# Paired down projections by seven block products: where the weight differences are kept, and weight chunks loaded in halves

## The reference

```
h2 = modulate(rms_norm(x, g_pre_ffn), shift_f, scale_f)
ff = (silu(h2 @ w_ffn_gate) * (h2 @ w_ffn_up)) @ w_ffn_down
x  = x + gate_f * rms_norm(ff, g_post_ffn)
```

## Time and profile before

| | |
|---|---|
| median of 3 runs | 2852.0 us (2851.5 to 2852.65) |
| the profiled execution's own time | 2855.09 us |
| its span, first to last instruction | 2853.3 us |
| PE busy | 2725.7 us, 96% |
| DVE busy | 1694.5 us, 59% |
| POOL busy | 1648.9 us, 58% |
| ACT busy | 903.4 us, 32% |
| pair stage, units 1 to 22 | 2273.7 to 2739.3 us of the span |

### The profile page before, as it was taken

How to read it: one execution, slowest core, us unless ns; L and a number is a source line. 1 busy time by engine, 2 the same in 40 slices (tenths; PEclk the granted TensorE clock), 3 DMA queues, 4 the chain that set the end, 5 groups by cost and what they waited for, 6 DMA issues and landing times.

```text
span 2853.3 us, 38214 instructions
## 1 busy us (share of the span) xinstructions
PE 2725.7 (96%) x13018; PEld 2165.8 (76%) x13018; DVE 1694.5 (59%) x2404; ACT 903.4 (32%) x1776; POOL 1648.9 (58%) x1253
## 2 busy tenths in 40 slices
PE   8999999898999999999999999989999999999988
PEld 5777777686878888887788887768777787777767
DVE  6666687747567777777633203665274456556647
ACT  5544444535211111214222125553242122121112
POOL 4566311366987777765433252213458977777764
PEclk9999999999999999999999999999999999999999
DMA  4322221044111121133411342213433111111124
GB/s 143 100 89 90 89 89 52 8 148 159 38 60 52 47 64 44 59 115 128 173 45 51 97 159 82 82 34 140 152 117 114 33 59 45 45 59 44 44 97 169
DMA packets 76676, 243.35 MB, mean 85 GB/s; under 512 B 7135, under 2 KB 11008, under 8 KB 76164
## 3 DMA queue, kind: packets, MB, share of 16 engines
q1 hardware_dynamic: 54464, 183.78, 20.3%
q10 hardware_dynamic: 22084, 57.86, 5.7%
HBM read 206.48 MB, written 32.52 MB: 84 GB/s over the span
## 4 chain that ended last, share of the span: by engine, by line
PE 67%; POOL 11%; DVE 9%; issue 5%; DMA 3%; ACT 3%; POOLq 0%; SPq 0%; ACTq 0%; DVEq 0%
PE ps L1036 15%; PE ps L1038 14%; PE ps L1037 14%; PE ps L1358 3%; PE ps L1359 3%; PE ps L1360 3%; DMA raw<-weights 3%; POOL raw L925 3%; PE ps L1127 2%; POOL wh L920 2%; PE ps L1143 2%; POOL wl L922 2%; POOL wl L913 1%; PE ps L1703 1%; PE ps L1715 1%
## 5 line engine op out<-in xcount | busy, mean ns | idle before, releaser
L771 POOL CAST wh<-raw 128x1024 fp32r<-128x1024 f32 x173 | 186.9, 1080 | 838.1 <-PE ps L1038 777.1
L1036 PE MATMUL ps<-hh,wh 128*128 128x512 f32 x1456 | 599.3, 412 | 15.6 <-DVE hl L2828 11.1
L1038 PE MATMUL ps<-hh,wl 128*128 128x512 f32 x1456 | 571.5, 393 | 0.0
L1037 PE MATMUL ps<-hl,wh 128*128 128x512 f32 x1456 | 570.4, 392 | 0.0
L773 POOL TENSOR_TENSOR wl<-raw,wh 128x1024 fp32r<-128x1024 f32 x173 | 416.7, 2409 | 13.9
L1036 PEld LDWEIGHTS ps<-hh,wh 128*128 128x128 f32 x1456 | 275.3, 189 | 87.5 <-issue 15.5
L1038 PEld LDWEIGHTS ps<-hh,wl 128*128 128x128 f32 x1456 | 274.7, 189 | 59.9
L1037 PEld LDWEIGHTS ps<-hl,wh 128*128 128x128 f32 x1456 | 275.9, 189 | 51.9 <-issue 3.3
L3121 DVE TENSOR_TENSOR arena<-ps,arena 128x512 f32<-128x512 f32 x288 | 195.8, 692 | 23.6 <-PE ps L1038 23.6
L865 POOL TENSOR_TENSOR wl<-raw,wh 128x512 fp32r<-128x512 f32 x136 | 189.5, 1393 | 10.9
L1036 PE MATMUL ps<-gated,wh 128*128 128x512 f32 (+1 forms) x464 | 178.7, 385 | 2.9 <-DVE gated L2919 2.6
(11 more groups left out here) (398 smaller groups left out, 5993.2 us busy)
## 6 DMA issues: line engine op xcount, KB each, us to landing
raw<-weights SPq DMA_DIRECT2D x270, 512.0 KB, 3.5
arena<-w_ada SPq DMA_DIRECT2D x48, 512.0 KB, 3.7
arena<-gate_scratch ACTq DMA_DIRECT2D x20, 512.0 KB, 4.6
arena<-x_t ACTq DMA_DIRECT2D x1, 4096.0 KB, 14.1
x_scratch<-arena ACTq DMA_DIRECT2D x2, 2048.0 KB, 8.9
arena<-x_scratch SPq DMA_DIRECT2D x2, 2048.0 KB, 10.7
gate_scratch<-arena ACTq DMA_DIRECT2D x16, 256.0 KB, 2.2
x_scratch<-arena ACTq DMA_DIRECT2D x1, 4096.0 KB, 14.0
```

Of the source, the lines that this page charges most:

```text
L771: pool.tensor_copy(wh[:, s], raw[:, r]).then_inc(Z.wt_hi, 1)
L1036: pe.matmul(out, wh[:, slot, w], xh, start=start, stop=False)
L1037: pe.matmul(out, wh[:, slot, w], xl, start=False, stop=False)
L1038: return pe.matmul(out, wl[:, slot, w], xh, start=False, stop=stop)
```

## The change

1. The difference b12 - b11 goes to a new place `T1_SUM` = `T(23)[:, HI]` instead of over b11. The differences that went over b21 go to `weight_sum`. Only b12 is still written over.
2. Each chunk of units 1 to 22 is loaded as two transfers of 256 KB, four a unit, with semaphores of their own for the second halves. Each is issued when POOL is done with what lies there: b11 after the unit's first difference; b21 after its last reader; b12 after the low half made from it; b22 after the last low half, as before.
3. In up units (the `else` branch of `pair_unit`, which the diff shows) the low half of block 2 is made ahead of block 1's (`UP_RANK` tells PE which count to wait for), and POOL waits for b12 and b22 separately. In down units the order of two differences is turned.
4. In the tail, the first chunk's loads wait for an earlier point; the value products of the last tiles use `T(23)[:, LO]` alone, with a wait on the unit before.

```diff
+        T1_SUM = T(23)[:, HI]
+        UP_RANK = (0, 2, 1, 3, 4, 5, 6)
-            def pair_load(k, ks, part):
-                sp.wait_ge(R.unit_split, unit_split(1, 0, (6, 8)[part]) if ks == 1 else up_split(k, 5 + part) - ST_BLOCKS)
+            def pair_load(k, ks, part, half):
+                c, r, w = (k - ks) * 2 + pair_chunk(ks, part), pair_chunk(ks, part) % RAW, (LO, HI)[half]
+                sp.dma_start(raw[:, r, w], src[:, w]).then_inc(pair_loaded(0, 0, part, half)[0], 16)
+            def pair_loads(k, ks):
...
+                down = ks % 3 == 1
+                sp.wait_ge(R.unit_hi, up_ops(k) - 8 + 1)
+                pair_load(k, ks, 0, 0)
+                if down:
+                    sp.wait_ge(R.unit_hi, up_ops(k) - 8 + 4)
+                    pair_load(k, ks, 0, 1)
+                    sp.wait_ge(R.unit_split, up_split(k, 3) - ST_BLOCKS)
+                    pair_load(k, ks, 1, 0)
+                else:
+                    sp.wait_ge(R.unit_split, up_split(k, UP_RANK[1]) - ST_BLOCKS)
+                    pair_load(k, ks, 1, 0)
+                    sp.wait_ge(R.unit_hi, up_ops(k) - 8 + 6)
+                    pair_load(k, ks, 0, 1)
+                sp.wait_ge(R.unit_split, up_split(k, 6) - ST_BLOCKS)
+                pair_load(k, ks, 1, 1)
...
-                sp.wait_ge(R.unit_split, up_split(LAST_UP, 5))
+                sp.wait_ge(R.unit_hi, up_ops(LAST_UP) + 6)
                 tail_load(0)
...
                 else:
                     direct_low(0, 0, b11)
-                    second_chunk()
+                    if ks == 1:
+                        pool.wait_ge(Z.a_lo, ST_DONE)
+                    loaded(1, 0)
                     pool.wait_ge(R.unit_split, up_split(k, 0))
-                    weight_sub(b11, b12, b11)
+                    weight_sub(T1_SUM, b12, b11)
+                    direct_low(2, 1, b21)
+                    loaded(1, 1)
                     pool.wait_ge(R.unit_hi, ops + 1)
                     weight_sub(b12, b22, b12)
                     part(1, b12, 2, 3)
-                    direct_low(2, 1, b21)
-                    weight_sub(weight_sum[:], b22, b11)
+                    weight_sub(weight_sum[:], b22, T1_SUM)
                     part(3, weight_sum[:], 4, 5)
-                    pool.wait_ge(R.unit_split, up_split(k, 2))
-                    weight_sub(b21, b21, weight_sum[:])
-                    part(4, b11, 6, 7)
-                    part(5, b21, 7, 8)
+                    pool.wait_ge(R.unit_split, up_split(k, 3))
+                    weight_sub(weight_sum[:], b21, weight_sum[:])
+                    part(4, T1_SUM, 1, 7)
+                    part(5, weight_sum[:], 6, 8)
                 direct_low(6, 2, b22)
...
-                    pe.wait_ge(R.unit_split, up_split(k, i))
+                    pe.wait_ge(R.unit_split, up_split(k, UP_RANK[i]))
...
-                pace(*pair_loaded(k, ks, 1 if j == 2 else 0))
+                pace(*pair_loaded(k, ks, *(((0, 1), (0, 0), (1, 1)) if down else ((0, 0), (0, 1), (1, 1)))[j]))
...
+                if group == 3 and u % 2:
+                    dve.wait_ge(Z.h_lo, 4 * group + u)
```

More of the change, by code:

```diff
@@ L206, in build @@
         sg_dram = nc.dram_tensor("gate_scratch", (20, P, S), F32, kind="Internal").ap()
-        Reused = namedtuple("Reused", "x_sum x_hi x_lo copied c_sum unit_split unit_done unit_hi x_out0 x_out1 a21_out a21_in x_back0 x_back1 mask_out mask_back lin_first cols_in x_in3 x_in4 first_h0 first_sc w_cast")
+        Reused = namedtuple("Reused", "x_sum x_hi x_lo copied c_sum unit_split unit_done unit_hi x_out0 x_out1 a21_out a21_in x_back0 x_back1 mask_out mask_back lin_first cols_in x_in3 x_in4 first_h0 first_sc w_cast half21 half22")
         R = Reused(lin_first=Z.d_exp, x_sum=Z.s_u, x_hi=Z.s_b, x_lo=Z.s_a, copied=Z.s_c, c_sum=Z.d_w, unit_split=Z.o_hi, unit_done=Z.z_full,
                    unit_hi=Z.o_lo, x_out0=Z.x_in0, x_out1=Z.x_in1, a21_out=Z.x_in2, a21_in=Z.mask_in, x_back0=Z.x_re,
-                   x_back1=Z.tab, mask_out=Z.e_out, mask_back=Z.bias_in, cols_in=Z.pos_in, x_in3=Z.so_in2, x_in4=Z.so_in3, first_h0=Z.trig_sin, first_sc=Z.m_tp, w_cast=Z.w_qk)
+                   x_back1=Z.tab, mask_out=Z.e_out, mask_back=Z.bias_in, cols_in=Z.pos_in, x_in3=Z.so_in2, x_in4=Z.so_in3, first_h0=Z.trig_sin, first_sc=Z.m_tp, w_cast=Z.w_qk, half21=Z.gate0, half22=Z.gate1)
         block = ctx.enter_context(nc.Block())
@@ L394, in unit_value @@
             i, half = T_UNITS[u]
-            return T(23)[:, half_of(1 - i)] if group == 3 else CV[i][:, half_of(half)]
+            return T(23)[:, LO] if group == 3 else CV[i][:, half_of(half)]
         def unit_gated(group, u):
@@ L619, in pair_raw, with pair_loaded @@
             return raw[:, r, LO], raw[:, r, HI]
-        def pair_loaded(k, ks, part):
+        def pair_loaded(k, ks, part, half):
             c = pair_chunk(ks, part)
+            if half and ks != LAST_DOWN:
+                return (R.half21, R.half22)[part], k * 16 + 32 * (KT // 2)
             return (Z.raw0, Z.raw1)[c % RAW], (k - ks) * 16 + 16 * (c // RAW + 1)
@@ L714, in st_chunks @@
                     sp.dma_start(MASK_BITS, MASK_DRAM).then_inc(R.mask_back, 16)
-            def pair_load(k, ks, part):
-                c, r = (k - ks) * 2 + pair_chunk(ks, part), pair_chunk(ks, part) % RAW
-                sp.wait_ge(R.unit_split, unit_split(1, 0, (6, 8)[part]) if ks == 1 else up_split(k, 5 + part) - ST_BLOCKS)
-                sp.dma_start(raw[:, r], A.w[c] if isinstance(c, int) else A.w[bass.ds(c, 1)].rearrange("a p n -> p (a n)")).then_inc(
-                    (Z.raw0, Z.raw1)[r], 16)
+            def pair_load(k, ks, part, half):
+                c, r, w = (k - ks) * 2 + pair_chunk(ks, part), pair_chunk(ks, part) % RAW, (LO, HI)[half]
+                src = A.w[c] if isinstance(c, int) else A.w[bass.ds(c, 1)].rearrange("a p n -> p (a n)")
+                sp.dma_start(raw[:, r, w], src[:, w]).then_inc(pair_loaded(0, 0, part, half)[0], 16)
+            def pair_loads(k, ks):
+                if ks == 1:
+                    for part in range(2):
+                        sp.wait_ge(R.unit_split, unit_split(1, 0, (6, 8)[part]))
+                        for half in range(2):
+                            pair_load(k, ks, part, half)
+                    return
+                down = ks % 3 == 1
[13 more added lines that the diff above has]
+                pair_load(k, ks, 1, 1)
             def tail_load(n):
@@ L731, in pair_chunks @@
                 for ks in range(1, 5):
-                    for part in range(2):
-                        pair_load(ks, ks, part)
+                    pair_loads(ks, ks)
                 with sp.Fori(0, PAIR_LOOPS) as i:
                     for ks in range(5, 11):
-                        for part in range(2):
-                            pair_load(i * 6 + ks, ks, part)
-                sp.wait_ge(R.unit_split, up_split(LAST_UP, 5))
+                        pair_loads(i * 6 + ks, ks)
+                sp.wait_ge(R.unit_hi, up_ops(LAST_UP) + 6)
                 tail_load(0)
@@ L747, in pair_chunks @@
                 for n in range(2):
-                    sp.wait_ge(R.unit_split, up_split(LAST_DOWN, 5 + n))
+                    if n == 0:
+                        sp.wait_ge(R.unit_hi, up_ops(LAST_DOWN) + 4)
+                    else:
+                        sp.wait_ge(R.unit_split, up_split(LAST_DOWN, 6))
                     tail_load(6 + n)
@@ L925, in weight_sub, with loaded @@
                     pool.tensor_tensor(dst, p, q, ALU.subtract).then_inc(R.unit_hi, 1)
-                def second_chunk():
-                    pool.wait_ge(*pair_loaded(k, ks, 1))
+                def loaded(part, half):
+                    pool.wait_ge(*pair_loaded(k, ks, part, half))
                     pool.sem_inc(Z.pace, 1)
@@ L933, in pair_unit @@
                     direct_low(1, 1, b11)
-                    second_chunk()
-                    pool.wait_ge(R.unit_split, up_split(k, 1))
-                    weight_sub(b11, b12, b11)
+                    loaded(1, 0)
+                    pool.wait_ge(R.unit_split, up_split(k, 0))
+                    weight_sub(T1_SUM, b12, b11)
+                    loaded(1, 1)
                     pool.wait_ge(R.unit_hi, ops + 1)
-                    weight_sub(weight_sum[:], b22, b11)
+                    weight_sub(weight_sum[:], b22, T1_SUM)
                     part(2, weight_sum[:], 2, 3)
+                    pool.wait_ge(R.unit_split, up_split(k, 2))
+                    weight_sub(weight_sum[:], b21, weight_sum[:])
                     weight_sub(b12, b22, b12)
-                    part(3, b12, 4, 5)
-                    pool.wait_ge(R.unit_split, up_split(k, 0))
-                    weight_sub(b21, b21, weight_sum[:])
-                    part(4, b21, 6, 7)
-                    part(5, b11, 7, 8)
+                    part(3, b12, 5, 6)
+                    part(4, weight_sum[:], 4, 7)
+                    part(5, T1_SUM, 1, 8)
```

(8 more changed lines are left out.)

## The result

| | before | after |
|---|---|---|
| median | 2851.75 us (4 runs, 2849.78 to 2852.65) | 2809.78 us (4 runs, 2807.57 to 2810.76) |
| ratio after / before | | 0.9853, 95% interval 0.9836 to 0.987 |
| span of the profiled execution | 2853.3 us | 2805.7 us |
| pair stage, units 1 to 22 | 465.6 us | 421.7 us |
| from the last up unit to the end | 114.0 us | 114.1 us |

The kernel is 42 us faster, 1.5%. The two profiled spans differ by 47.6 us. Of that, 43.9 lie in the pair stage. So the 3.8 us are scatter between executions, and the stage's 43.9 is the figure to compare with the 42 of the medians.

What follows compares the result with a forecast made beforehand. POOL's stall at unit starts was taken to bound the kernel, starving PE; 42.0 us from triples two to seven plus 2.1 from the last up unit, together 44, gave 2852.0 - 44 = 2808 us, range 2803 to 2824.

Steps and rivals of the forecast that it cites:

- its stall at each unit's start: Pair stage: POOL waits 3.34 us for ACT's high half from newly landed weights, making its unit 21.2 us against PE's 19.17.
- POOL's unit without the stall: Pair stage: POOL's work stays 17.84 us a unit, 53.5 a triple against PE's 57.5, leaving 4 us of slack a triple.
- b22's loop: Pair stage: 13.9 us from POOL getting b22 to releasing it, plus L, stays within PE's 19.17 while L is below 5.3.
- L: Time from the end of a unit's last low half to POOL's start on the newly loaded b22; taken as 3 us.
- The turned order: Up units: block 1's low half comes one instruction (1.25 us) later, hidden by the ring, so it costs nothing.
- the cover of about 5 us: Up units: block 1, the tightest, is ready at 16.5 us after PE's start and wanted by PE at 21.8.
- The clock: Pair stage: eight matmuls slow down after a 1.94 us stall, 8 us in all, which goes with the stalls.
- The tail at nothing: After the last up unit: PE's wait for the chunk behind the two reloads stays, so the tail gains nothing.
- The sum of 44 us: Pair stage: 42.0 us saved in triples two to seven plus 2.1 in the last up unit.
- what sets the down unit: Down units: DVE's 28 additions, 19.34 us against 19.04 of PE's matmuls, were said to set the length.
- the 57.50: Microseconds of the first, unstalled triple (252 matmuls), taken as the model for all the others.
- the lead that POOL brings in: Pair stage: POOL's head start at entry, which keeps the first triple unstalled and is lost at some 2 us a unit.

Runs made afterwards that it cites:

- e1: Changed kernel with differences still outside the raw buffers, but each chunk loaded as one whole 512 KB transfer again: 2824.59 us, ratio 0.9907.
- e2: Half loads issued as halves come free, but with the differences in place and the order of the kernel before: 2823.54 us, ratio 0.99.
- e7: Changed kernel with one more POOL instruction a unit, the first difference repeated once on 256 columns: 2808.27 us, ratio 0.9848.
- e8: Changed kernel with two more POOL instructions a unit, the first difference repeated twice on 512 columns: 2833.01 us, ratio 0.9937.
- e4: Changed kernel with b22's load issued only after the second low half of the unit it belongs to: 2829.25 us, ratio 0.9926.
- e3: Changed kernel with block 2's low half made after block 1's again in up units (UP_RANK the identity): 2807.2 us, ratio 0.9851.
- e5: Changed kernel with the tail's second and third weight chunks issued ahead of the two 1 MB reloads: 2798.39 us, ratio 0.9812.
- e6: Changed kernel with DVE's 28 down-unit additions done on 256 of 512 columns, leaving work out: 2804.94 us, measured once.
- e9: Changed kernel with the address of `sums` moved by 32 bytes to a multiple of 64: 2807.98 us, ratio 0.9844.

## Why the prediction was right, by its steps

- **What bounded the kernel** (POOL, by its stall at each unit's start): shown. e1 and e2 leave parts of the stall in and lose 15 and 14 us of the 42; with it gone PE never waits.
- **POOL's unit without the stall, 17.84 us, and its slack of 1.33**: shown by e7 and e8 on either side.
- **b22's loop, 13.9 + L below 5.3**: right. The half landed in 2.6 us, 3.3 at most, and e4 shows L itself, 2.9 us, where I took 3. e4 also moved the loop past the bound, with the stalls worked out. The rule of the Trainium skill on batching (DMA: Bandwidth & Descriptors, Bandwidth) would have kept whole chunks. The Trainium skill's formula (same page, Anatomy of one DMA, a fit for transfers that GpSimd issues) gives 2.6 us for a half, which the trace shows, and 3.2 for a whole, where the trace before has 3.7. e1 shows that whole chunks are slower here by 15 us: what counts is when a buffer is free again, and the stage moves only 46 to 56 GB/s.
- **The turned order costs nothing**: right, with the cover of about 5 us as worked out, and e3 adds that it brings nothing. The prediction calls the unit from which it counts, unit 10, a second up unit; it is the first of its triple, and the working holds for that one.
- **The clock**: the 8 us of matmuls at the lower level went with the stalls, and the stage stood at 1.00. With PE's 26.4 us of idle time they make 34 of the 44 us. The other 10 come with the waits too, some 0.35 us for each of the 28: a wait of PE costs more than its idle time. In e1, e2, e4 and e8, where the clock never fell, a wait cost 0.3 to 0.4 us beyond it. Prediction and result both have this in the windows' difference.
- **The tail at nothing**: right, 114.0 us before and 114.1 after. e5 shows the cause that was named, the chunk's place behind the reloads.
- **The sum of 44 us**: 43.9 in the profile, 42.0 between the medians.
- **Wrong: what sets the down unit.** I said that DVE's 28 additions do, since 19.34 us lie so near to the 19.40. e6 refutes it, and in e9 the down unit takes 19.23 us with all 28 additions whole. DVE's additions follow the matmuls one by one, so their sum takes PE's time, not the other way. It cost the forecast nothing, because the first triple carried the 57.50 as measured, whatever its cause.
- In the expectations for the experiments the lead that POOL brings in was taken at 7 us. The losses measured leave 5 in e1 and e8, 7 in e4 and 11 in e2. The windows show how long it lasts: two triples at 57.5 us in e1 and e2, one in e4 and e8. Why it lasts longest in e2, which then loses 3.4 us a triple, is open.

## What to carry to other kernels

When a producer with spare capacity still starves the bound engine, look for the loop through its input buffer: last use, transfer, first use. Its price is the work between getting and releasing the last piece plus the landing time; free each piece at its last reader, by writing derived data elsewhere and loading in pieces, until this falls below the bound engine's period, and no further. A stretch of the same kernel in which the bound engine didn't wait served here as the model of the result, and it held although the reason given for its length was wrong. A sum of durations near a period is no proof that they set it: ask who waits for whom inside it.

## What the runs showed of the hardware

- With its moving operand (`sums`) starting 32 bytes beyond a multiple of 64, a down unit of 84 matmuls, 48 of which stream it, took 19.40 us; moved by 32 bytes, it took 19.23. The three groups' means went from 396, 395 and 395 ns to 394, 389 and 392 (e9).
- Waits of PE of up to 1.3 us, two to four a triple, left the granted clock at 1.00 (e1, e2, e4, e8). In the kernel before it fell to the lower of its two levels, for about eight matmuls each time, after five of the six waits of 1.76 to 1.94 us, and after the tail's 8.3 for ten.
- A wait of PE cost 0.3 to 0.4 us more than its idle time (e1: 14.4 us lost in the stage with 9.8 of idle time in 12 waits; e8: 24.0 with 18.7 in 18).
- A load of 256 KB landed in 2.6 us (2.4 to 3.3) where one of 512 KB took 3.7 (3.4 to 4.9): half the bytes for 70% of the time.
